# Preparation of the recurrent layer placed between its gate tiles, with the decay tile ahead of them

## The reference

```python
def _gdn_mixer(h, conv_prev, s0, w_in, w_conv, a_log, dt_bias, o_norm, w_out):
    proj = h @ w_in                       # q, k, v (3072), gate (1024), a_in (8), b_in (8)
    ...
    conv = jax.nn.silu(conv)              # causal convolution over 4 tokens of q, k, v
    new_conv = xp[:, t_len:]              # last 3 rows before the convolution, an output
    ...
    beta = jax.nn.sigmoid(b_in)
    g = -jnp.exp(a_log) * jax.nn.softplus(a_in + dt_bias)
    o, s_new = _gated_delta_chunked(q, k, v, g, beta, s0)
    o = _rms_norm(o, o_norm) * jax.nn.silu(gate)
    return o @ w_out, new_conv, s_new
```

## Time and profile before

| what | us |
|---|---|
| median of 3 runs | 2928.45 |
| lowest and highest | 2926.96, 2937.08 |
| profiled execution, its own time | 2925.1 |
| its span | 2923.2 |
| PE busy | 2786.8 (95%) |
| DVE busy | 1381.4 (47%) |
| ACT busy | 945.3 (32%) |

### The profile page before, as it was taken

How to read it: one execution, slowest core, us unless ns; L and a number is a source line. 1 busy time by engine, 2 the same in 40 slices (tenths; PEclk the granted TensorE clock), 3 DMA queues, 4 the chain that set the end, 5 groups by cost and what they waited for, 6 DMA issues and landing times.

```text
span 2923.2 us, 49947 instructions
## 1 busy us (share of the span) xinstructions
PE 2786.8 (95%) x20760; PEld 2667.7 (91%) x20760; DVE 1381.4 (47%) x1739; ACT 945.3 (32%) x1351; POOL 272.1 (9%) x308
## 2 busy tenths in 40 slices
PE   8999999997999799999999999999988989999998
PEld 7999999995888599999999999999976679999997
DVE  4434347745545454343464344333546844343354
ACT  4222134434333232121233232222336833222234
POOL 2000002201233310000011000000120010000011
PEclk9999999998999799999999999999998989999999
DMA  5232222210011222322222332322212333222221
GB/s 133 72 86 86 76 78 91 81 57 20 17 32 31 75 73 85 87 86 74 74 83 72 110 111 83 86 86 73 85 44 80 109 101 87 84 74 86 83 73 65
DMA packets 307351, 225.65 MB, mean 77 GB/s; under 512 B 8526, under 2 KB 300799, under 8 KB 307199
## 3 DMA queue, kind: packets, MB, share of 16 engines
q1 hardware_dynamic: 306512, 224.26, 25.5%
q0 software_dynamic: 576, 0.00, 0.0%
q10 hardware_dynamic: 162, 0.04, 0.0%
HBM read 212.14 MB, written 12.13 MB: 77 GB/s over the span
## 4 chain that ended last, share of the span: by engine, by line
PE 87%; DVE 7%; ACT 3%; issue 1%; POOL 1%; DMA 1%; SPq 0%; DVEq 0%; POOLq 0%; ACTq 0%
PE ps L490 77%; PE ps L1474 2%; PE ps L1423 1%; DVE ls L1797 1%; DVE ls L1804 1%; POOL dx L725 1%; DVE w_lo L451 1%; DVE ls_lo L1811 0%; PE ps L1334 0%; ACT att L1698 0%; DVE xt L1102 0%; PE ps L2030 0%; PE ps L1220 0%; PE ps L1482 0%; PE ps L2781 0%
## 5 line engine op out<-in xcount | busy, mean ns | idle before, releaser
L490 PE MATMUL ps<-hx_hi,w_hi 128*128 128x320 f32 (+1 forms) x3986 | 859.5, 297 | 12.6 <-DVE hx_lo L2150 7.1
L490 PE MATMUL ps<-hx_lo,w_hi 128*128 128x320 f32 (+1 forms) x3986 | 859.2, 296 | 0.0
L490 PE MATMUL ps<-hx_hi,w_lo 128*128 128x320 f32 (+1 forms) x3986 | 844.7, 293 | 0.0
L441 ACT ACTIVATE w_hi<-raw 128x1024 fp32r<-128x1024 f32 (+2 forms) x378 | 381.9, 1012 | 1284.3 <-PE ps L490 1279.3
L490 PEld LDWEIGHTS ps<-hx_hi,w_hi 128*128 128x128 f32 x3986 | 604.8, 188 | 15.4 <-issue 7.0
L490 PEld LDWEIGHTS ps<-hx_lo,w_hi 128*128 128x128 f32 x3986 | 616.0, 190 | 0.0
L490 PEld LDWEIGHTS ps<-hx_hi,w_lo 128*128 128x128 f32 x3986 | 609.2, 188 | 0.0
L451 DVE TENSOR_TENSOR w_lo<-raw,w_hi 128x1024 fp32r<-128x1024 f32 (+2 forms) x378 | 469.3, 1242 | 113.8 <-ACT w_hi L441 113.6
L490 PE MATMUL ps<-hid_hi,w_hi 128*128 128x320 f32 (+1 forms) x1664 | 358.5, 297 | 12.8 <-DVE of L1198 8.3
L490 PE MATMUL ps<-hid_lo,w_hi 128*128 128x320 f32 (+1 forms) x1664 | 357.6, 297 | 0.0
L490 PE MATMUL ps<-hid_hi,w_lo 128*128 128x320 f32 (+1 forms) x1664 | 356.3, 295 | 0.0
(11 more groups left out here) (408 smaller groups left out, 2394.6 us busy)
## 6 DMA issues: line engine op xcount, KB each, us to landing
raw<-in_ffn_w_in SPq DMA_DIRECT2D x176, 512.0 KB, 5.0
raw<-in_ffn_w_out SPq DMA_DIRECT2D x64, 512.0 KB, 4.4
raw<-in_a_w_in SPq DMA_DIRECT2D x33, 512.0 KB, 4.4
raw<-in_ffn_w_out SPq DMA_DIRECT2D x32, 384.0 KB, 3.5
raw<-in_ple_w_gate SPq DMA_DIRECT2D x16, 512.0 KB, 4.1
raw<-in_w_kv SPq DMA_DIRECT2D x16, 512.0 KB, 3.9
k_page<-in_cache_k SPq DMA_DIRECT2D x16, 512.0 KB, 3.3
v_page<-in_cache_v SPq DMA_DIRECT2D x16, 512.0 KB, 4.7
```

Source lines behind the costliest of these rows:

```text
L441: nc.scalar.activation(w_hi[:, m, 0:k], s.view(m, slot), ACT.Copy).then_inc(w_hi_done, 1)
L490: last = nc.tensor.matmul(TILE[m][:, c0:c1], w[:, m, k], h[:, k, c0:c1], start=k == 0 and a == 0, stop=k == k_all - 1 and a == 2)
```

## The change

Order of the products: the unit `ab` comes first and holds the decay tile and gate tile 0; then three units with gate tiles 1 to 6; then a unit with gate tile 7 alone (`alone`) and the unread slice. The preparation no longer stands in `gdn_*`. It is cut into functions that the gate units call, `gates_pe` between the tiles on PE, `ab_act`, `gate_act`, `ab_dve` and `gate_dve` on ACT and DVE.

The square sums go in four batches of four tiles. Tile j of a batch is squared into a buffer of its own (of eight: free gate tiles, `sqb`, `ssum`, `std`), and its matmul writes PSUM partitions 32j to 32j+31 with 32 weight columns of `hot`; the four groups are added at the end by `norm_rows`. PE runs batch 0 to 3 after gate tiles 0 to 3, the transposes of decays after tile 2, decay sums after tile 3, square norms and rows by head after tile 4. `new_rows` moves to the end of `raw`, its transposes to after gate tiles 6 (16) and 7 (8); the first 16 wait for the last unit's weight splits. `stored` is waited for later, ahead of `vb_s`.

```diff
         product("qkv", CT // 2, KD, KD, pair_loads(w_a, 0), HX, stats=True)
-        product("gate", HA // 2, KD, KD, pair_loads(w_a, QKV), HX)
-        product("ab", 1, KD, 1, two_loads(w_a, AB0, w_a, AB0, KD, 1), HX)
+        product("ab", 1, KD, KD, two_loads(w_a, AB0, w_a, QKV, KD, KD), HX)
+        product("gate", HA // 2 - 1, KD, KD, pair_loads(w_a, QKV + P), HX, first=1)
+        product("gate", 1, KD, 1, two_loads(w_a, QKV + (HA - 1) * P, w_a, AB0, KD, 1), HX, first=HA - 1, alone=True)
...
+        squared = [gates[:, HA // 2 + j] for j in range(4)], [sqb[:, 0], sqb[:, 1], ssum[:], std[:]]
+        sum_s, std16 = gates[:, HA - 2], gates[:, HA - 1]
+        SQUARE_SUMS = ps[:, 6:8, 0:HC]
...
+        def square(act, c):
+            b, j = c // 4, c % 4
+            act.wait_ge(conv_done, 2 * c + 2)
+            if b >= 2:
+                act.wait_ge(g["summed"], b - 1)
+            nc.scalar.activation(squared[b % 2][j], qkv[:, c], ACT.Square).then_inc(g["square"], 1)
...
+        def ab_act(act, s, N, split):
+            for c in range(0, 4):
+                square(act, c)
+            split_hi(act, split, 0)
+            act.wait_ge(rs_done, s.n["stat"])
+            done("e32r", nc.scalar.activation(e32_r[:], e32[:], ACT.Copy))
+            for c in range(4, 8):
+                square(act, c)
+            softplus_exp(act)
+            split_hi(act, split, 1)
+            act.wait_ge(evac[1], N + 1 - (s.n["unit"] - s.n["eb"]))
+            nc.scalar.activation(gates[:, 0], up_s[:], ACT.Silu).then_inc(silu_done, 1)
+            act.wait_ge(evac[0], N + 1)
+            done("sg", nc.scalar.activation(sg[AB_ROWS], ab[AB_ROWS], ACT.Sigmoid))
+
+        def gate_act(act, s, N, u, m, split):
+            tile = s.first + 2 * u + m
+            if s.alone:
+                move_rows(act, new_rows_step, 1, range(0, 4))
+            split_hi(act, split, m)
+            act.wait_ge(evac[m], N + 1 - m * (s.n["unit"] - s.n["eb"]))
...
+            nc.scalar.activation(gates[:, tile], (gate_s, up_s)[m][:], ACT.Silu).then_inc(silu_done, 1)
+            if tile in (1, 2):
+                for c in range(4 + 4 * tile, 8 + 4 * tile):
+                    square(act, c)
+            if tile == 4:
+                after(act, "norms")
+                done("std16", nc.scalar.activation(halves(std16[0:2 * HA]), STAT[0:2 * HA], ACT.Sqrt, bias=eps[0:2 * HA]))
+            if tile == 5:
+                rows_high(act)
+            if tile == 6:
+                decay_exps(act)
+            if s.alone:
+                move_rows(act, new_rows_step, 1, range(4, 6))
...
+        def gate_dve(dve, s, N, u, m, split):
+            tile = s.first + 2 * u + m
+            if s.alone:
+                move_rows(dve, new_rows_step, 0, range(0, 4))
+            dve.wait_ge(tile_done, 2 * N + m + 1)
+            dve.wait_ge(silu_done, s.n["gs"] + 2 * u + m - 1)
+            nc.vector.tensor_tensor((gate_s, up_s)[m][:], TILE[m], rs[:], ALU.mult).then_inc(evac[m], 1)
+            split_lo(dve, split, m)
+            if tile == 2:
+                token_columns(dve)
+            if tile == 3:
+                decay_columns(dve)
+            if tile == 4:
+                rows_by_head(dve)
+            if tile == 6:
+                rows_low(dve)
+            if s.alone:
+                beta_columns(dve)
+                move_rows(dve, new_rows_step, 0, range(4, 6))
+
+        def square_sums(pe, b):
+            pe.wait_ge(g["square"], 4 * b + 4)
...
+            for half in range(2):
+                for j in range(4):
+                    c = 4 * b + j
+                    last = nc.tensor.matmul(SQUARE_SUMS[32 * j:32 * j + 32, half], hot[:, 15 - c:47 - c],
+                                            squared[b % 2][j][:, half * HC:(half + 1) * HC], start=b == 0, stop=b == 3, skip_group_check=True)
+            last.then_inc(g["summed"], 1)
...
+        def norm_rows(pe):
+            after(pe, "squares", "cst0", "cst1")
+            for half in range(2):
+                last = nc.tensor.matmul(STAT[0:2 * HA, half], e32[:, 0:2 * HA], sum_s[:, half * HC:(half + 1) * HC], start=True, stop=True)
+            done("norms", last)
...
+        def gates_pe(pe, s):
+            for u in range(s.units):
+                for m in range(2):
+                    multiply(pe, s, u, m)
+                    tile = s.first + 2 * u + m - (s.kind == "ab")
+                    if 0 <= tile < 4:
+                        square_sums(pe, tile)
+                    if tile == 2:
+                        ab_by_token(pe)
+                    if tile == 3:
+                        decay_sums(pe)
+                    if tile == 4:
+                        norm_rows(pe)
+                        decay_rows(pe)
+                    if tile == 6:
+                        after(pe, "std16", "rows_gcs", "rows_bes")
+                        pe.wait_ge(new_done, 2 * CT)
+                        pe.wait_ge(w_lo_done, 2 * (s.n["unit"] + s.units) + 2)
+                        turn_rows(pe, new_rows_step, range(0, 4))
+                    if tile == HA:
+                        turn_rows(pe, new_rows_step, range(4, 6))
```

More of the change, by code:

```diff
@@ L32, in __init__ @@
     def __init__(self, kind, stats=False, after=None, sums=False, fills=(), layer=0, units=0, ka=0, kb=0, loads=None,
-                 view=None, rhs=None, dst=None, scale=1.0, coef=1.0, end=False):
+                 view=None, rhs=None, dst=None, scale=1.0, coef=1.0, end=False, first=0, alone=False):
         self.kind = kind
@@ L44, in __init__ @@
         self.end = end
+        self.first, self.alone = first, alone
         self.n = {}
@@ L382, in program @@
             count["unit"] += s.units
-            count["eb"] += s.units if s.kind != "ab" else 0
+            count["eb"] += s.units - s.alone
             count["tok"] += len(s.fills)
@@ L392, in program @@
                 count["hid"] += s.units
-            if s.kind in ("gu", "ple", "gate"):
-                count["gs"] += s.units * (1 if s.kind == "gu" else 2)
+            if s.kind in ("gu", "ple", "gate", "ab"):
+                count["gs"] += s.units * (1 if s.kind in ("gu", "ab") else 2) - s.alone
             if s.kind == "ple":
@@ new lines, in rows_high, with decay_exps @@
+        def rows_high(act):
+            for name, p0, n in (("rows_gc", 32, HA), ("rows_be", 64, HA), ("rec", 0, 2 * HA)):
+                after(act, name)
+                done(f"rhi{p0}", nc.scalar.activation(rows_hi[p0:p0 + n], rows[p0:p0 + n, 0:TP], ACT.Copy))
+        def decay_exps(act):
+            after(act, "cst0", "cst1", "kdx0", "kdx1")
+            done("ex0", nc.scalar.activation(est[:, 0:C_S], cst[:, 0:C_S], ACT.Exp))
+            done("ex1", nc.scalar.activation(est[0:TS, C_S:], cst[0:TS, C_S:], ACT.Exp))
+            done("exk0", nc.scalar.activation(kdc[:, 0:C_E], kdc[:, 0:C_E], ACT.Exp))
+            done("exk1", nc.scalar.activation(kdc[0:TS, C_E:], kdc[0:TS, C_E:], ACT.Exp))
@@ new lines, in decay_columns, with rows_by_head @@
+        def decay_columns(dve):
+            after(dve, "sums_by_token")
+            done("cst0", nc.vector.tensor_copy(cst[:, 0:C_S], bank(5)[:, 0:C_S]))
+            done("cst1", nc.vector.tensor_copy(cst[0:TS, C_S:], bank(5)[0:TS, C_S:C_S + 2 * HA]))
+            dve.wait_ge(g["summed"], 4)
+            done("squares", nc.vector.tensor_copy(halves(sum_s), SQUARE_SUMS))
+        def rows_by_head(dve):
+            after(dve, "gc_all")
+            for name, p0 in (("gc", 32), ("be", 64)):
+                done("rows_" + name, nc.vector.tensor_copy(rows[p0:p0 + HA, 0:TP], bank(6)[p0:p0 + HA]))
+                done(f"rows_{name}s", nc.vector.tensor_copy(rows[p0:p0 + HA, TP:T], bank(7)[p0:p0 + HA, 0:TS]))
+            after(dve, "std16")
+            done("rec", nc.vector.reciprocal(rows[0:2 * HA], std16[0:2 * HA]))
@@ new lines, in ab_by_token, with decay_sums @@
+        def ab_by_token(pe):
+            after(pe, "g", "sg")
+            for i in range(NT):
+                n = P if i < PT else TS
+                for half, src in enumerate((rows, sg)):
+                    last = nc.tensor.transpose(ps[0:n, 4, (2 * i + half) * NR:(2 * i + half + 1) * NR], src[RB:P, i * P:i * P + n],
+                                               ident[RB:P, RB:P])
+            done("tok_ab", last)
+        def decay_sums(pe):
+            mm = nc.tensor.matmul
+            after(pe, "tokc0", "tokc1")
+            gp = tokc[:, 0:PT, C_G:C_G + HA]
+            gs_ = tokc[0:TS, PT, C_G:C_G + HA]
+            mm(ps[:, 5, 0:C_E], triu[:], gp, start=True, stop=True)
+            mm(ps[:, 5, C_E:C_S], ones[:], gp, start=True, stop=True)
+            mm(ps[0:TS, 5, C_S:C_S + HA], triu_s[:], gs_, start=True, stop=True)
+            done("sums_by_token", mm(ps[0:TS, 5, C_S + HA:C_S + 2 * HA], same[:], gs_, start=True, stop=True))
@@ new lines, in norm_rows, with decay_rows @@
+        def norm_rows(pe):
[3 more added lines that the diff above has]
```

(20 more changed lines are left out.)

218 lines of the change are left out of this document (87 added, 131 removed).

## The result

| | before | after |
|---|---|---|
| median on the same chip, us | 2932.76 | 2908.22 (6 runs, 2903.17 to 2914.96) |
| ratio | | 0.9918, interval 0.9906 to 0.993 |
| profiled execution, us | 2925.1 | 2911.09 |
| its span, us | 2923.2 | 2909.4 |
| forecast, us | | 2904.6 (2899 to 2917) |

What follows compares the result with a forecast made beforehand. PE, busy 95%, was taken as the bound, so only time without product tiles counts: 19.2 + 2.45 + 2.2 = 23.85 us off 2925.1 gives 2901.2, plus 3.35 to the median: 2904.6 us, range 2899 to 2917.

Steps and rivals of the forecast that it cites:

- What goes, what comes back: End of the gate stage: 33.37 us without tiles leave, 14.15 us return between tiles on PE; recurrent layer 19.2 us earlier.
- the wait for `w_lo`: Ahead of gate tile 7, PE's first 16 transposes wait for the last unit's weight splits, costing 1.0 us.
- the wait for the last row copies: At the end of the stage PE waits until DVE has moved out the last new rows, 0.9 us.
- Covers: ACT and DVE preparation hides under the gate tiles at no cost; smallest cover 2.0 us, at the third squares.
- rival 2: Table switches on ACT cost as much again; PE waits 2.6 us for the third squares, total 2907.2 us; 8%.
- The products for the sample rows: Start of recurrent layer: DVE's four sample-row products start together with PE's spread, gaining another 2.45 us.
- The clock at the layer's start: Start of recurrent layer: full tiles until 673 keep PE's clock at 1.00, so two DVE waits on PE, 2.2 us, vanish.
- From profile to median: Profile forecast 2901.2 us plus the 3.35 us by which the median exceeds the profiled execution gives 2904.6 us.
- rival 1: Square-sum column groups run one after the other on PE, so 11.7 us come back, 2916.3 us; 12%.
- 3: Gain inside the recurrent layer does not come, sample-row products and waits on PE stay; 4.65 us, 2909.3 us; 6%.
- 4: Clock dips after each of seven lumps between gate tiles, 11.2 us; with the 2.2 us 2918.0 us; 10%.
- 5: Clock, once fallen, stays at half through the gate tiles, 6.35 us more per tile, 2962 us for all nine; 4%.

Runs made afterwards that it cites:

- e1_one_group: Changed kernel with all square sums written to one group of 32 PSUM partitions instead of four; 2919.66 us, ratio to the kernel before 0.9968.
- e4_busy: Changed kernel with 17 useless matmuls in PE's gaps at the start of the recurrent layer; 2905.89 us, ratio to the kernel before 0.9928.
- e3: Changed kernel with eight more unread squares of 440 columns on ACT ahead of the third batch of squares; 2911.34 us, ratio to the kernel before 0.9948.
- e2: Kernel before, preparation left at the end of the stage, with four column groups, eight square buffers and the fold; 2929.61 us, ratio 1.0001.
- e6: Changed kernel with the weight-split wait moved from PE to ACT and DVE, last 8 transposes ahead of the unread slice; 2904.61 and 2905.16 us, ratios 0.9898 and 0.9906.

## Why the prediction was right, and where it was not

- **What goes, what comes back.** Right. The first spread was forecast 19.2 us earlier, and is 18.8. The terms: a lump 1.31 us (forecast 1.11; it is the 1.18 of the records plus 0.13 of change-over); the wait for `w_lo` 1.14 (1.0); the wait for the last row copies 1.01 (0.9); the piece with rows by head and fold 2.65 (3.36). The last was too high because the fold (L862) and the first half of the rows by head (L869) overlap, as their interleaved records at 648.82 to 649.07 show; they write different groups of partitions, but so they do in e1_one_group, where they don't overlap, so what makes them overlap is open. The errors cancel: about 14.5 us in all for 14.15.
- **Covers.** Right. ACT, which I had finishing the third squares 2.0 us ahead of PE, finished them at 629.8 us and PE came to them at 631.95, without a wait. ACT's timeline of the kernel after also bears on rival 2:

```profile
619.32 1.28 ACT L721 ACT_TABLE_LOAD   x1
620.61 0.69 ACT L721 ACTIVATE gates<-up_s 128x576 f32<-128x576 f32 x1
621.32 1.28 ACT L723 ACT_TABLE_LOAD   x1
622.61 0.68 ACT L723 ACTIVATE sg<-ab 32x576 f32<-32x576 f32 x1
```

  A load takes 1.28 us and the next operation starts 0.01 us behind it, also where two come close together. Rival 2 had PE wait 2.6 us for the third squares; it waited for none, so rival 2 falls. The Trainium skill, "ScalarE: Activation LUTs", section "What ACT_TABLE_LOAD costs", adds a drain of about 1.38 us to each switch; this trace shows none, only the 0.01 us.
- **The products for the sample rows.** Right: 21.57 us earlier, forecast 19.2 + 2.45 = 21.65.
- **The clock at the layer's start.** Wrong. I had the clock at 1.00 and the two waits of DVE, 2.2 us, gone. It fell at 679, and the waits are 0.42 + 2.67 = 3.1 us, 0.9 more than before. The step that failed is "full tiles run until 673, so I expect 1.00 there": it took what stands ahead of the layer for the cause. The runs show that full tiles ahead of it are not enough: the fall came 3.1 us behind the first spread, behind a stretch of thin spreads with PE busy 2.08 of 2.68 us and within a wait of 1.10 us, and all profiles with the preparation between the tiles have it. What at the layer's start brings it stays open; e4_busy doesn't settle it. At `xt` this left 20.6 us of the 23.85.
- **From profile to median.** Not argued well enough. I took before's profile as typical of its runs and after's as 3.35 us under its median. Before's profile was a short one, half of its runs are 8 us longer, and what the clock term lacked (3.1 us) came back by that. So the total fits better than its steps: 22 to 23 us over all runs for 23.85 forecast. That is luck, as far as the clock goes.
- **Rivals.** 1 is refuted by the 1.18 us and is what e1 built (2919.7 us; rival 1 said 2916.3). 3 is half true: L1102 came early, the waits stayed. 4 and 5 are refuted by 1.00 over all of 603.99 to 676.10. Yet e3 shows that 5 had a door: one wait of 2.5 us and the clock fell in the middle of dense tiles, though for less than 8 us and not for the rest.

## What to carry to other kernels

A serial preparation of one engine's thin work belongs between dense tiles when the other engines have room beside them; here 33 us of it cost 14.5 there. Give its matmuls different groups of output partitions (here they were worth 12.5 us of the stretch, e1), but only where they don't wait for their input: in the old place the same groups gave nothing (e2). A wait of PE between tiles can cost about twice its length, when the clock falls with it (one profile, e3), so put a wait for a place on the engine that writes it, not on PE (e6, 1.6 us). Before subtracting two profiles, look whether either kernel's runs lie in heaps, profile more than one execution of each, and compare places, from a common zero point, not spans.

## What the runs showed of the hardware

- Eight fp32 matmuls with 32 weight columns and 288 columns each, in four groups of output partitions, took 1.18 us, in one group 4.07. Matmuls of different code can overlap too (L862 with L869, 128 partitions read by both), but in e1_one_group, where L862 reads 32, the same two did not, and that took 0.97 us more.
- The clock kept 1.00 through 27 us of square sums with PE busy 21.6 of 27.1, and was at 0.52 behind e2's first 6.7 us, with PE busy 3.33 of them.
- It fell in a stretch in which PE shows no idle (e4, 684 to 688), with thin spreads and useless products mixed. The cause stays open.
- Both kernels have short falls in the recurrent layer, some in every profile of a kernel (at 711 in the changed one) and some in one execution and not in another (at 786). In before they make 7.4 and 8.0 of the 10.0 and 11.0 us by which two long executions exceed a short one. Their cause is open too.
